# Loading x for the residual into the residual stream itself, ten of seventeen tiles ahead of the output projection

## What is computed

```python
def layer(x, p_l, ...):
    hn = rmsnorm(x, g_mix)
    z = hn @ w_in                                    # u, b, c, h and two gates
    ...
    merged = sigmoid(gp) * (pool_out @ w_pool_up) + sigmoid(gc) * (conv_out @ w_conv_out)
    x = x + merged @ w_o
    hn = rmsnorm(x, g_ffn)
    gu = hn @ w_ffn_in
    x = x + (silu(gu[..., :D_FF]) * gu[..., D_FF:]) @ w_ffn_out
    x = x + sigmoid(rmsnorm(x, g_ple) @ w_ple_gate) * (p_l @ w_ple)
```

## Time and profile before

| | us |
|---|---|
| median of 3 runs | 981.04 (979.98 to 981.09) |
| the profiled execution's own time | 980.72 |
| its span on the slowest core, core 2 | 979.2 |
| spans of cores 0 to 7 | 970.7, 977.1, 979.2, 979.1, 976.4, 974.3, 970.0, 977.4 |

### The profile page before, as it was taken

How to read it: one execution, slowest core, us unless ns; L and a number is a source line. 1 busy time by engine, 2 the same in 40 slices (tenths; PEclk the granted TensorE clock), 3 DMA queues, 4 the chain that set the end, 5 groups by cost and what they waited for, 6 DMA issues and landing times.

```text
span 979.2 us, 14991 instructions; the slowest of 8 cores (970.0 to 979.2 us)
## 1 busy us (share of the span) xinstructions
PE 941.1 (96%) x4984; PEld 456.6 (47%) x4984; DVE 447.7 (46%) x560; ACT 269.4 (28%) x546; POOL 254.6 (26%) x294
## 2 busy tenths in 40 slices
PE   7887999999999989999999999999999999998995
PEld 5533445554444534444444444444444444443442
DVE  3377654422222338626428224522632362164986
ACT  4552644322222224320110110011011101165543
POOL 1044454343333321010100110011211440057242
PEclk9898999999999999999999999999999999999998
DMA  8917535077233389662062353073935620025333
GB/s 268 319 59 150 100 39 49 11 98 85 27 28 27 42 187 282 146 71 27 6 71 22 44 60 27 1 81 28 142 46 71 63 46 1 1 59 120 135 135 130
DMA packets 138892, 80.93 MB, mean 83 GB/s; under 512 B 118895, under 2 KB 121583, under 8 KB 138800
## 3 DMA queue, kind: packets, MB, share of 16 engines
q0 software_dynamic: 77312, 38.35, 30.6%
q1 hardware_dynamic: 60832, 41.10, 15.5%
q10 hardware_dynamic: 672, 0.52, 0.2%
HBM read 87.71 MB, written 9.50 MB: 99 GB/s over the span
## 4 chain that ended last, share of the span: by engine, by line
PE 87%; DMA 4%; issue 3%; DVE 2%; POOL 1%; ACT 1%; DVEq 0%; POOLq 0%; SPq 0%; ACTq 0%
PE psum L90 87%; DMA t<-xp 3%; DVE t L90 2%; ACT t L90 1%; POOL t L90 1%; DMA t<-t 1%; POOL t L118 0%; DVEq L140 0%; DVEq L101 0%; POOLq L140 0%; ACTq L101 0%; SPq L118 0%; POOLq L101 0%; POOLq L117 0%; ACT L90 0%
## 5 line engine op out<-in xcount | busy, mean ns | idle before, releaser
L90 PE MATMUL psum<-t,t 128*128 128x512 bf16 (+2 forms) x4856 | 931.5, 355 | 25.0 <-DVE t L90 13.3
L90 PEld LDWEIGHTS psum<-t,t 128*128 128x128 bf16 x4856 | 447.1, 99 | 509.0 <-issue 37.5
L90 DVE TENSOR_TENSOR t<-psum,t 128x1024 f32<-128x1024 f32 (+5 forms) x375 | 315.6, 845 | 481.5 <-PE psum L90 431.9
L90 ACT ACTIVATE t<-psum 128x512 f32<-128x512 f32 (+6 forms) x288 | 149.6, 533 | 577.9 <-PE psum L90 572.1
L90 POOL TENSOR_TENSOR t<-t,t 128x1 f32<-128x1 f32 (+4 forms) x93 | 112.8, 1221 | 234.5 <-DVE t L90 176.4
L118 POOL DMA_DIRECT2D t<-w_ffn_in x44 | 38.8, 890 | 339.9 <-PE psum L90 339.5
L90 ACT ACTIVATE t<-t 128x1024 bf16<-128x1024 f32 (+6 forms) x158 | 95.5, 613 | 90.7 <-DVE t L90 67.8
L90 DVE SCALAR_TENSOR_TENSOR t<-t,t,t 128x512 f32<-128x512 f32 (+3 forms) x84 | 86.4, 1035 | 22.0 <-POOL t L90 7.9
L90 POOL TENSOR_TENSOR t<-t 128x526 f32<-128x526 f32 (+10 forms) x51 | 53.3, 1046 | 98.1 <-ACT t L90 92.9
L90 DVE TENSOR_TENSOR t<-t,t 128x1024 f32<-128x1024 f32 (+3 forms) x20 | 23.0, 1148 | 2.1
L90 ACT ACTIVATE t<-t,t 128x512 f32<-128x512 f32 (+2 forms) x21 | 14.0, 679 | 22.1 <-DVE t L90 22.1
(11 more groups left out here) (15 smaller groups left out, 20.0 us busy)
## 6 DMA issues: line engine op xcount, KB each, us to landing
t<-w_ffn_in POOLq DMA_DIRECT2D x44, 256.0 KB, 6.6
t<-xp SPq DMA_DIRECT2D x16, 512.0 KB, 15.0
t<-w_in SPq DMA_DIRECT2D x16, 512.0 KB, 15.5
t<-xp POOLq DMA_DIRECT2D x16, 512.0 KB, 5.5
yp<-t SPq DMA_DIRECT2D x16, 512.0 KB, 2.6
t<-w_in POOLq DMA_DIRECT2D x16, 256.0 KB, 7.6
t<-w_ffn_out POOLq DMA_DIRECT2D x4, 1024.0 KB, 12.6
t<-w_o POOLq DMA_DIRECT2D x1, 2048.0 KB, 15.7
```

Of the source, the lines that this page charges most:

```text
L90: fn = (lambda eng, meth=meth, kw=kw: getattr(eng, meth)(**kw))
```

## The change

The 17 tiles of x are loaded straight into `x_res` and the buffers `xin5` are gone; the DVE addition reads and writes the same place. A list `SG` says in which of the 17 places a tile lies, and every later use of `x_res` goes through it: tiles 0 to 9 lie in places 4 to 12 and 16, tiles 10 to 12 in places 13 to 15 and tiles 13 to 16 in places 0 to 3. Places 4 to 12 and 16 are those that nothing uses any more once the projections are done (`wres`, `ubuf`, `vbuf`, `tbuf`, norm buffers). Places 0 to 3 and 13 to 15 hold merge buffers and `wfuse` until the merge ends. All 17 loads are issued by SP, not POOL: ten are written between the merge's column blocks m = 3 to 7, two ahead of each, and seven behind the load of `g_ffn`.

```diff
     x_res, _ = sbt(A0, [128, NT, D], F32)
+    SG = list(range(4, 13)) + [16, 13, 14, 15, 0, 1, 2, 3]
...
+    Dxr = [em.newsem("dxr%d" % i) for i in range(NT)]
+
+    def xr_load(t):
+        em.dma("sp", x_res[:, SG[t], :], xtile(t), Dxr[t], writes=[Rx[t]])
+
+    for t in range(10):
+        Rx[t].inherit(*Rwp, *Ru, *Rv, *Rt, Rctm, Rctv, Rwgf, *Rxn1, *Rs4[14:])
     for m in range(2, 8):
+        if m >= 3:
+            xr_load(2 * m - 6)
+            xr_load(2 * m - 5)
         sl = s4_slots()
...
-    def s5_x(t):
-        if t < NT:
-            em.dma("pool", xin5[t % 4][:, :], xtile(t), Dxin5[t % 4], writes=[Rxin5[t % 4]])
...
-        em.op("dve", "tensor_tensor", dict(out=x_res[:, t, :], in0=psum[:, b0:b0 + 2, :].rearrange("p a b -> p (a b)"),
-                                           in1=xin5[t % 4][:, :], op=ALU.add),
-              reads=[Rps[b0], Rps[b0 + 1], Rxin5[t % 4]], writes=[Rx[t]])
-        s5_x(t + 4)
+        em.op("dve", "tensor_tensor", dict(out=x_res[:, SG[t], :], in0=psum[:, b0:b0 + 2, :].rearrange("p a b -> p (a b)"),
+                                           in1=x_res[:, SG[t], :], op=ALU.add),
+              reads=[Rps[b0], Rps[b0 + 1]], writes=[Rx[t]])
...
     em.dma("sp", gfb[:, :], g_ffn.partition_broadcast(128), Dgfb, writes=[Rgfb])
-    for t in range(4):
-        s5_x(t)
+    for t in range(10, NT):
+        xr_load(t)
```

More of the change, by code:

```diff
@@ L304, in build_nc @@
     o = C0 + 17408
[L305 to L308, removed]
     xn5 = []
@@ L314, in build_nc @@
     gfb, o = sbt(C0, [128, D], F32)
-    for i in range(2):
-        t_, o = sbt(o, [128, D], F32)
-        xin5.append(t_)
     junk5, o = sbt(o, [128, D], BF16)
@@ L1162, in build_nc @@
         w_done(*sl)
-    Rxin5 = [Res() for _ in range(4)]; Dxin5 = [em.newsem("dxin5%d" % i) for i in range(4)]
     Rxn5 = [Res() for _ in range(4)]
@@ L1168, in build_nc @@
     allpo = [Rpo[k][tb] for k in range(4) for tb in range(5)]
-    for r_ in Rxin5[0:2] + Rxn5:
+    for r_ in Rxn5:
         r_.inherit(*allco)
-    for r_ in Rxin5[2:4] + [Rj5, Rgfb]:
+    for r_ in [Rj5, Rgfb]:
         r_.inherit(*allpo)
-    alls4 = Rs4 + Rwp + Ru + Rv + Rt + Rwf + [Rctm, Rctv, Rwgf] + Rxn1
-    for t in range(NT):
-        Rx[t].inherit(*alls4)
-    def s5_x(t):
-        if t < NT:
-            em.dma("pool", xin5[t % 4][:, :], xtile(t), Dxin5[t % 4], writes=[Rxin5[t % 4]])
+    for t in range(10, NT):
+        Rx[t].inherit(*(Rs4 + Rwp + Ru + Rv + Rt + Rwf + [Rctm, Rctv, Rwgf] + Rxn1))
     def s5_a(t):
@@ L1197, in build_nc @@
             s5_a(k)
-            st5[k] = norm_stat(x_res[:, k, :], Rx[k], junk5, Rj5)
+            st5[k] = norm_stat(x_res[:, SG[k], :], Rx[k], junk5, Rj5)
         if k >= 1:
@@ L1202, in build_nc @@
             em.op("dve", "reciprocal", dict(out=rs, in_=ms), reads=[Rms], writes=[Rrs])
-            em.op("dve", "scalar_tensor_tensor", dict(out=xn5[t % 4][:, :], in0=x_res[:, t, :], scalar=rs, in1=gfb[:, :],
+            em.op("dve", "scalar_tensor_tensor", dict(out=xn5[t % 4][:, :], in0=x_res[:, SG[t], :], scalar=rs, in1=gfb[:, :],
                                                       op0=ALU.mult, op1=ALU.mult),
@@ L1210, in build_nc @@
         for tb in range(5):
-            Ract[fl][tb].inherit(*allpo, Rgfb, Rj5, *Rxin5[2:4])
+            Ract[fl][tb].inherit(*allpo, Rgfb, Rj5)
     Rsg6 = [Res(), Res()]; Rxn6 = [Res() for _ in range(4)]; Rj6 = Res()
     for r_ in Rsg6 + Rxn6 + [Rj6]:
-        r_.inherit(*allco, *Rxin5[0:2], *Rxn5)
+        r_.inherit(*allco, *Rxn5)
     Rwfo = [Res(), Res()]; Dwfo = [em.newsem("dwfoa"), em.newsem("dwfob")]
@@ L1278, in s6_out @@
               lambda k, half, wi=wi: wfo[wi][:, k, half * 512:(half + 1) * 512], [Rwfo[wi]], nf)
-        em.op("dve", "tensor_tensor", dict(out=x_res[:, t, :], in0=psum[:, b0:b0 + 2, :].rearrange("p a b -> p (a b)"),
-                                           in1=x_res[:, t, :], op=ALU.add),
+        em.op("dve", "tensor_tensor", dict(out=x_res[:, SG[t], :], in0=psum[:, b0:b0 + 2, :].rearrange("p a b -> p (a b)"),
+                                           in1=x_res[:, SG[t], :], op=ALU.add),
               reads=[Rps[b0], Rps[b0 + 1]], writes=[Rx[t]])
@@ L1294, in s6_norm_steps @@
                 if 0 <= k - 1 < NT:
-                    st6[k - 1] = norm_stat(x_res[:, k - 1, :], Rx[k - 1], junk6, Rj6)
+                    st6[k - 1] = norm_stat(x_res[:, SG[k - 1], :], Rx[k - 1], junk6, Rj6)
                 t = k - 2
@@ L1299, in s6_norm_steps @@
                     em.op("dve", "reciprocal", dict(out=rs, in_=ms), reads=[Rms], writes=[Rrs])
-                    em.op("pool", "tensor_tensor", dict(out=xn6[t % 4][:, :], in0=x_res[:, t, :], in1=rs.to_broadcast([128, D]), op=ALU.mult),
+                    em.op("pool", "tensor_tensor", dict(out=xn6[t % 4][:, :], in0=x_res[:, SG[t], :], in1=rs.to_broadcast([128, D]), op=ALU.mult),
                           reads=[Rx[t], Rrs], writes=[Rxn6[t % 4]])
@@ L1348, in s7_b @@
         em.op("dve", "tensor_tensor",
-              dict(out=x_res[:, t, cs], in0=x_res[:, t, cs], in1=tt7[i][:, cs], op=ALU.add),
+              dict(out=x_res[:, SG[t], cs], in0=x_res[:, SG[t], cs], in1=tt7[i][:, cs], op=ALU.add),
               reads=[Rtt7[i][h] for h in rr], writes=[Rx[t]] if t != LAST else [Rxl[h0]])
@@ L1358, in s7_c1 @@
         Rms = Res(); Rrs = Res()
-        em.op("act", "activation", dict(out=junk[:, :], in_=x_res[:, t, :], func=AF.Square, scale=1.0 / 32.0, accum_out=ms),
+        em.op("act", "activation", dict(out=junk[:, :], in_=x_res[:, SG[t], :], func=AF.Square, scale=1.0 / 32.0, accum_out=ms),
               reads=[Rx[t]], writes=[Rjunk, Rms])
@@ L1365, in s7_c2 @@
         rs, Rrs = s7rs[t]
-        em.op("dve", "scalar_tensor_tensor", dict(out=x_res[:, t, :], in0=x_res[:, t, :], scalar=rs, in1=gfin[:, :],
+        em.op("dve", "scalar_tensor_tensor", dict(out=x_res[:, SG[t], :], in0=x_res[:, SG[t], :], scalar=rs, in1=gfin[:, :],
                                                   op0=ALU.mult, op1=ALU.mult),
               reads=[Rrs, Rgfin], writes=[Rx[t]])
-        em.dma("sp", ytile(t), x_res[:, t, :], Dyo[t % 8], reads=[Rx[t]], final=True)
+        em.dma("sp", ytile(t), x_res[:, SG[t], :], Dyo[t % 8], reads=[Rx[t]], final=True)
     for k in range(NT):
@@ L1389, in last_sq @@
         cs = slice(h * 512, (h + 1) * 512)
-        em.op("act", "activation", dict(out=junk[:, cs], in_=x_res[:, LAST, cs], func=AF.Square, scale=1.0 / 32.0, accum_out=msl[h]),
+        em.op("act", "activation", dict(out=junk[:, cs], in_=x_res[:, SG[LAST], cs], func=AF.Square, scale=1.0 / 32.0, accum_out=msl[h]),
               reads=[Rxl[h]], writes=[Rjunk, Rml[h]])
@@ L1407, in build_nc @@
         cs = slice(h * 512, (h + 1) * 512)
-        em.op("dve", "scalar_tensor_tensor", dict(out=x_res[:, LAST, cs], in0=x_res[:, LAST, cs], scalar=rsl, in1=gfin[:, cs],
+        em.op("dve", "scalar_tensor_tensor", dict(out=x_res[:, SG[LAST], cs], in0=x_res[:, SG[LAST], cs], scalar=rsl, in1=gfin[:, cs],
                                                   op0=ALU.mult, op1=ALU.mult),
               reads=[Rrs, Rgfin, Rml[h]], writes=[Rxl[h]])
-        em.dma("sp" if h == 0 else "act", ytile(LAST)[:, cs], x_res[:, LAST, cs], Dyo[(LAST + 3 * h) % 8], reads=[Rxl[h]], final=True)
+        em.dma("sp" if h == 0 else "act", ytile(LAST)[:, cs], x_res[:, SG[LAST], cs], Dyo[(LAST + 3 * h) % 8], reads=[Rxl[h]], final=True)
     assert wst["taken"] == len(WL) and wst["issued"] == len(WL), wst
```

## The result

The changed kernel takes 983.9 us (median of 10 runs, 982.03 to 985.41) where the kernel before, run beside it, takes 980.76. The ratio is 1.0031, with a 95% interval of 1.0022 to 1.0041: slower by 0.3%, more than the 0.2% that can be told from no change. The prediction was 980.8, no change, in the range of 976.4 to 984.4, with 0.22 on slower.

What follows compares the result with a forecast made beforehand. PE bounds the kernel, busy in 941.1 of 979.2 us. Core 3 without the gap, 974.9, plus 2.4 wait and 1.7 clock gives 979.0; plus 1.5 and 0.3 to the median, 980.8 us, range 976.4 to 984.4.

Steps and rivals of the forecast that it cites:

- The gap at 355 us: PE idle plus lower clock while DVE waits for x, 350 to 362 us; removal put core 3 at 974.9.
- the case without a collision: Faster rival: w_conv_out for m = 3 lands before 235.6 or under 1 us after; 976.7 us, chance 0.38.
- That nothing holds the ten loads back: In SP's list only the first early load waits, so all ten go out behind the ncs stores, not spread.
- The collision's place and mechanism: Ten x loads just ahead of w_o and w_conv_out for m = 3 delay those columns, wanted at 235.6.
- The wait's size: PE's wait at m = 3 on core 3, taken as the middle between 0 and 4.8, some 2.4 us.
- The upper bound: If all DMA work adds up, columns for m = 3 land at 240.4 and PE stands for 4.8 us.
- full addition: Ten x loads, 16.1 us at 326 GB/s, less 4.0 us of idle engines, all delay the m = 3 columns.
- the 326 of the earlier trace: GB/s for x alone with engines busy throughout; makes the ten early loads 16.1 us of DMA time.
- The clock: Lower clock after the wait at m = 3: the same 1.7 us lost as at the removed gap.
- The slower rival: Wait at m = 3 with all adding up, x at 300 GB/s: 6.2 + 1.7 us, time 984.6, chance 0.22.
- The late loads in front of the transposes: Seven x loads ahead of the first transpose in SP's queue: late by a microsecond or two, put at nothing.
- PE's four tiles of lead, 14 us, hide that: In the output projection, PE's lead covers a first transpose late by a microsecond or two; cost nothing.

Runs made afterwards that it cites:

- e1: Changed kernel with POOL issuing the load of w_o behind the weights of the next column block, not ahead of them: 976.5 us, ratio 0.9948.
- e2: Changed kernel with each pair of early x loads waiting for POOL's last addition of the column block before, so really spread: 976.5 us, ratio 0.9944.
- e8: Changed kernel with both edits, early x loads gated to spread over m = 3 to 7 and w_o behind the weights of m = 3 and 4: 976.1 us.
- e3: Changed kernel with eight x tiles loaded early at m = 3, not ten, and nine late: 978.5 us, ratio 0.9966.
- e4: Changed kernel with five x tiles loaded early at m = 3, not ten, and twelve late: 976.5 us, ratio 0.9946.
- e6: Changed kernel with no x tile loaded early, all 17 issued from SP at the merge's end: 987.8 us, ratio 1.0057.
- e5: Kernel before, with POOL issuing the first four x loads ahead of the three feed-forward weight loads at the merge's end: 986.6 us, ratio 1.0047.
- e7: Changed kernel with the ten early x loads at once, ungated, ahead of the small stores in SP's queue: 983.5 us, ratio 1.0017.

## Why the prediction was off

**The gap at 355 us** was priced at 4.2 us on core 3 and 5.2 on core 2. With everything else out of the way (e1, e2, e8) the kernel takes 976.1 to 976.5; the case without a collision was put at 976.7. The step held, but that the numbers are so close is partly luck: in e1 and e2 core 3 ended at 972.8 and 972.3 us, not 974.9, and another core was the slowest. From 80 to 100 us, far from the change, PE stood on core 3 for 6.0 us in the run before and for 4.3 and 3.8 in these two.

**That nothing holds the ten loads back** held: one row of ten loads in 5.7 us, issued at 206.7 (predicted 206.3). But their data did not follow at once, as the prediction had it ("in data from about 206.6"): on core 3 q1 moved 0.12 MB from 206 to 209 us, 0.09 of it behind 208.4.

**The collision's place and mechanism** held: the columns of `w_conv_out` for m = 3, behind `w_o`. e1 removes the one half of the sum from in front of them and e2 the other, and each removes the whole wait.

**The wait's size** is the step that failed: "I take the middle between 0 and 4.8, some 2.4 us". Measured were 5.3 us on core 3. The upper bound was no bound but nearly the value. It said 240.4 for the landing; core 3 issued `w_o` 1.5 us earlier in this execution than before, which makes 238.9, and the chain of waits of after has the load from 209.97 for 29.16 us, to 239.1. What I held against full addition was that x had been seen at 377 GB/s for a microsecond, and that x might pass beside short packets for nothing. Neither helped. Core 3 of after, 211 to 223 us:

```profile
q1 hardware_dynamic: 656, 2.38, 58.2%
q0 software_dynamic: 379, 0.78, 40.9%
```

`w_o` is read as 4-byte and written as 2-byte numbers, so 0.78 MB written are 1.56 read. The core reads 2.38 + 1.56 = 3.94 MB in 12 us, 328 GB/s (from 213 us on, with both at work, 1.66 + 1.56 MB, 322 GB/s), and the engines are busy for 99% of it: whatever time one takes is missing for the other. For this shared stretch the 326 of the earlier trace rows, a mean over five microseconds, was the rate to use and not the best single one.

That the bound fits to 0.2 us is partly luck, though. While x was alone, from 209 to 213 us, it ran faster than 326: 1.45 MB in 4 us, 363 GB/s, on core 3, and 400 on core 2. Against that, its data began 1.8 us later than assumed and `w_o` came only 2.4 us behind it, not 4.3, so that it found less idle time. The two errors about cancelled.

**The clock** was the second half of the miss: "so I add the same 1.7 us of lower clock". The lower level lasted 6.8 us on core 3, not 3.4, of which 1.9 lay in the wait itself; PE lost 2.5 us by it. Together: forecast 2.4 + 1.7 = 4.1 us on core 3, measured 5.3 + 2.5 = 7.8, 3.7 us more. Core 3 ended only 2.7 us later than forecast (981.7 for 979.0), since it was 1.5 us ahead at `w_o` already; the 0.5 left over is not explained. The slowest core was core 1, which ended at 982.4: its wait of 4.6 and 2.8 us of clock make 7.4, which is what e1 and e2 gained over the changed kernel (983.9 to 976.5).

**The slower rival** had the right mechanism and, by luck, the right sum, 6.2 + 1.7 = 7.9 us, from two wrong terms: a rate of 300 GB/s that was too low for the shared stretch, and a loss to the clock that was too small. Its chance of 0.22 was too low: of the bounds of the wait, only the upper one rested on a stretch of several microseconds.

**The late loads in front of the transposes** held for seven (0.2 us of DVE's wait, none of PE's). But "PE's four tiles of lead, 14 us, hide that" is close to an edge, as e3, e4 and e6 show: two more late loads make 6.3 us of DVE's wait, and with ten more PE stands for 8.2 us.

## What to carry to other kernels

Ask of a transfer that was moved to a free queue what that queue still waits for: where the text interleaves it with a loop that is another engine's, it is issued at once. Then add its time, at the rate of a long stretch and in bytes read, to whatever is in flight there, and look for the first small load behind the large one. Mend it by order, small and soon wanted ahead of large and late, or by a gate on the loop's progress; here either turned 0.3% slower into 0.5% faster.

Where a transfer is first in the critical chain, look also at who comes next in the same queues: without the early loads, having x sooner only moved the wait to the transposes (e5, e6).

## What was not expected of the hardware

- The granted clock can fall while PE still stands, and only the part of the lower level that outlasts the stop costs anything. How long it lasts grew with the stop, by no fixed relation: not at all after 1.9 us idle (cores 4 and 5 of before) and 2.2 (core 6 of after); 3.4 us after 2.1 to 3.5 (cores 1, 2, 3 and 7 of before, core 0 of after); 6.8 after 4.3 to 5.3 (cores 1, 2, 3, 5 and 7 of after), but also after 3.2 (core 3 of e5); some 10 after 8.2 (core 3 of e6). On core 2 of e6 5.9 us idle brought only 3.4. The loss of PE's time was 1.4 to 3.0 us in each of these, and no larger behind the longest stop (2.6 us).
- Two queues that both have work share by packets, not bytes: from 205 to 211 us of e7 422 packets of the one and 421 of the other, with 1.54 and 0.11 MB; from 215 to 230 us of after on core 3, 626 and 626. A weight load of short rows beside the long packets of x moves at a fraction of its pace.
